# A two-layer decoder step: kept cache rows copied from input to output in the feed-forward stage, and an earlier report of GpSimd to the stage barrier

## The reference, cut to what matters

```python
# per layer, sample group (8 sequences x 4 tokens)
win_buf = cache_win_kv[l]                                  # (8, 512, 2, 2, 64)
kw = jnp.concatenate([win_buf, kv_w], axis=1)              # 512 old rows, then 4 new ones
o_w = window_attn(q, kw, q_pos, k_pos)
s_win[l] = kw[:, -512:]                                    # output: rows 4..511 of the cache, then the 4 new rows
C_new = decay * C + einsum(ws, k, v)                       # recurrent state, (8, 4, 64, 128), an output too
x = x + g1 * (concat(a_out, m_out) @ wo)                   # output projection
u, gt = split(xn2 @ w_up); y = (silu(conv(u)) * gt) @ w_down
```

## Time and profile before

| | us |
|---|---|
| median of 3 runs | 1839.16 (1837.89 to 1844.75) |
| the profiled execution's own time | 1831.91 |
| its span, first to last instruction | 1830.1 |
| TensorE busy | 1698.8 (93%) |
| VectorE busy | 919.4 (50%) |
| ScalarE busy | 610.7 (33%) |
| GpSimd busy | 187.5 (10%) |

### The profile page before, as it was taken

The page is one execution under the profiler, slowest core; times in us unless marked ns, Lnnn a source line. Parts: engine busy times, 40 slices in busy tenths (PEclk is TensorE's granted clock), DMA queues, the critical chain, the costliest instruction groups (busy, mean ns, idle before and its releaser), DMA issues.

```text
span 1830.1 us, 37052 instructions
## 1 busy us (share of the span) xinstructions
PE 1698.8 (93%) x14719; PEld 1526.7 (83%) x14719; DVE 919.4 (50%) x2374; ACT 610.7 (33%) x1165; POOL 187.5 (10%) x304
## 2 busy tenths in 40 slices
PE   5899998977989999999989999898798999999996
PEld 4799965545989999999989997645598999999995
DVE  2534434646365645546463343474545554654644
ACT  2332225634142323323152212463333332422413
POOL 1001003432000000000000100153200000000001
PEclk9899988988989999999999997898898999999998
DMA  8335278369322222221133535634861222221201
GB/s 297 118 99 181 78 273 261 115 225 200 82 76 65 92 93 93 93 92 47 49 89 90 179 102 186 221 105 137 217 114 47 92 93 93 93 92 47 93 24 54
DMA packets 157903, 219.42 MB, mean 120 GB/s; under 512 B 11722, under 2 KB 116490, under 8 KB 157548
## 3 DMA queue, kind: packets, MB, share of 16 engines
q1 hardware_dynamic: 150096, 199.22, 34.7%
q0 software_dynamic: 7648, 17.94, 3.9%
HBM read 200.45 MB, written 16.68 MB: 119 GB/s over the span
## 4 chain that ended last, share of the span: by engine, by line
PE 85%; DVE 5%; ACT 3%; SPq 2%; issue 2%; DMA 1%; POOL 1%; DVEq 1%; ACTq 0%
PE ps L1237 28%; PE ps L1263 15%; PE ps L809 13%; PE ps L1197 6%; PE ps L683 2%; PE ps L920 2%; PE ps L935 2%; PE ps L854 2%; PE ps L890 1%; PE ps L795 1%; PE ps L804 1%; PE ps L803 1%; SPq L546 1%; PE ps L1217 1%; PE ps L870 1%
## 5 line engine op out<-in xcount | busy, mean ns | idle before, releaser
L1237 PE MATMUL ps<-work_r,big_r 128*128 128x272 f32 x1344 | 279.2, 289 | 1.4 <-ACT work L1622 0.3
L1237 PE MATMUL ps<-work_r,slab_r 128*128 128x272 f32 x1344 | 278.5, 288 | 0.0
L1237 PE MATMUL ps<-xnT_r,big_r 128*128 128x272 f32 x1344 | 276.4, 287 | 0.0
L1237 PEld LDWEIGHTS ps<-work_r,big_r 128*128 128x128 f32 x1344 | 210.2, 188 | 3.9 <-issue 3.9
L809 PE MATMUL ps<-slab_r,work_r 128*128 128x256 f32 (+1 forms) x976 | 213.3, 285 | 0.0
L1237 PEld LDWEIGHTS ps<-xnT_r,big_r 128*128 128x128 f32 x1344 | 211.7, 188 | 0.0
L1237 PEld LDWEIGHTS ps<-work_r,slab_r 128*128 128x128 f32 x1344 | 210.5, 188 | 0.0
L1727 DVE TENSOR_TENSOR slab_r<-slab,big_r 128x2048 fp32r<-128x2048 f32 (+1 forms) x84 | 170.2, 2036 | 49.5 <-ACT big_r L1606 44.1
L809 PEld LDWEIGHTS ps<-slab_r,work_r 128*128 128x128 f32 x976 | 163.4, 191 | 2.7 <-issue 2.5
L1625 ACT ACTIVATE big<-big,work 128x560 f32<-128x560 f32 x44 | 33.7, 765 | 372.1 <-DVE big L2321 372.1
L1263 PE MATMUL ps<-side_r,big_r 128*128 128x272 f32 x704 | 148.3, 292 | 4.9 <-DVE big_r L1727 4.9
(11 more groups left out here) (446 smaller groups left out, 3204.9 us busy)
## 6 DMA issues: line engine op xcount, KB each, us to landing
slab<-in_w_mod SPq DMA_DIRECT2D x23, 2048.0 KB, 9.0
slab<-in_w_up SPq DMA_DIRECT2D x44, 1024.0 KB, 7.5
slab<-in_w_in SPq DMA_DIRECT2D x20, 1024.0 KB, 5.9
slab<-in_w_down SPq DMA_DIRECT2D x20, 1024.0 KB, 6.0
slab<-in_cache_cmp_kv SPq DMA_DIRECT2D x128, 128.0 KB, 2.0
slab<-in_cache_sel_kv SPq DMA_DIRECT2D x96, 128.0 KB, 2.0
big<-in_cache_win_kv SPq DMA_DIRECT2D x16, 512.0 KB, 5.2
out<-big POOLq DMA_DIRECT2D x16, 448.0 KB
```

The costliest lines, as they stand in the source:

```text
L1237: ins = mm(ps[2 * half + b][:, 0:HALF], wt, fr(x[:, k, HALF * b:HALF * b + HALF]), start=k == 0 and n == 0, stop=k == KC - 1 and n == 2)
```

## The change

Three edits. The 16 stores of window rows from `big` in the decode part of each layer are gone; in their place 8 DMAs a layer copy the same rows from the input tensor to the output tensor, issued by GpSimd in the feed-forward part behind `decode_scaled`. GpSimd adds to `stage_done` right behind the `kwb` products, ahead of its waits for `ms_Cc` and its state stores, where before it did so behind them. ScalarE's wait ahead of `split_out(0)` goes, and with it the first of the three `win_kept` reports per layer; the semaphore is now `states_kept`, with two reports per layer.

```diff
-        ST_ALL = 16 * (3 + 2 + NB + 1 + NB + 2 + 16 + 8 + 2)
+        ST_ALL = 16 * (3 + 2 + NB + 1 + NB + 2 + NB + 8 + 2)
...
-        win_kept = ctx.enter_context(nc.semaphore("window_rows_and_states_stored"))
+        states_kept = ctx.enter_context(nc.semaphore("states_and_tails_stored"))
...
                 act.wait_ge(d_pv.sem, d_pv.at(4, L))
-                act.wait_ge(win_kept, 3 * L + 1)
                 split_out(0)
...
-                    dve.wait_ge(win_kept, 3 * L)
+                    dve.wait_ge(states_kept, 2 * L)
...
-                        dve.wait_ge(win_kept, 3 * L + 2)
+                        dve.wait_ge(states_kept, 2 * L + 1)
...
-                for b in range(NB):
-                    if b % 4 == 0:
-                        pool.wait_ge(wpg_in[b // 4], L * 64 + 64)
-                    ob = by_part(s_win[L][b][0:WINDOW - NT])
-                    for lo, hi in ((1, 113), (113, 128)):
-                        put(ob[lo - 1:hi - 1], wpg[b][lo:hi].rearrange("p i c -> p (i c)"))
                 pool.wait_ge(d_s.sem, d_s.at(6, L))
...
                 ins.then_inc(ms_kb.sem, 1)
-                all_stored()
-                pool.sem_inc(win_kept, 1)
+                pool.sem_inc(stage_done, 1)
                 for s_ in range(2):
...
-                pool.sem_inc(stage_done, 1)
                 pool.wait_ge(stage_done, stage_end(12, L))
...
                 all_stored()
-                pool.sem_inc(win_kept, 1)
+                pool.sem_inc(states_kept, 1)
                 decode_scaled(2 * L + 1, 24)
+                for b in range(NB):
+                    put(by_part(s_win[L][b][0:WINDOW - NT]), by_part(A["cache_win_kv"][L][b][NT:WINDOW]))
                 pool.wait_ge(ul_c.sem, ul_c.at(6, L))
...
                 all_stored()
-                pool.sem_inc(win_kept, 1)
+                pool.sem_inc(states_kept, 1)
```

## The result

The changed kernel took 1828.2 us in the median of 8 runs (1823.71 to 1831.36), the kernel before 1836.38 in the median of 8 beside it (1829.23 to 1844.75): a ratio of 0.995, 95% interval 0.9932 to 0.9968, or 8.2 us less. The forecast was 7.7 us less. The profiled execution took 1829.4 us and its span is 1827.1 us, so between the two profiled spans only 3.0 us show.

A forecast was written before the change was run, and what follows sets the result against it. TensorE, busy 93% of the span, bounds the kernel; gains come only where it stands still. Barrier 4.6 plus page wait 3.1, all else 0, makes 7.7 us: 1839.2 to 1831.5 us, range 1825.5 to 1839.5.

The forecast's parts named there:

- Barrier, 4.6 us: Barrier behind the decode part: GpSimd reports before its state stores, VectorE becomes last; 2.3 us gained per layer.
- ScalarE's wait, 0: Ahead of split_out(0) in the decode part: its weights' landing, not GpSimd, released the split, so removal gains nothing.
- Page wait, 3.1 us: Last selected page in the decode part: without window stores SyncE's loads speed up, ending TensorE's 1.46 and 1.64 us waits.
- The clock, 0: TensorE's half clock behind the barrier: its end might move along, stay or come sooner; taken as 0, between them.
- more than the sum: Rival, chance 0.13: shorter barrier pause restores TensorE's full clock at once, 2.2 us more per layer; 12.1 us gained, 1827.1.
- Copies, 0: Start of the feed-forward part: eight copies a layer, 4.16 MB in 14.5 us, run in idle DMA engines and cost nothing.
- the 24.5 us of room: Feed-forward part: idle DMA time between the copies' issue at about 519.3 and the next loads at 543.82.
- The slow-copies rival: Feed-forward up-projection loads: copies over 32 us run beside them, landing 11.1 us late; 14.5 us slower, 1853.7; chance 0.06.
- half shares: Up-projection loads beside copies: queues alternate by packet, load gets about half, takes 15 us, 3.6 us late per layer.

The follow-up runs named there:

- barrier_alone: The kernel before with only GpSimd's report to stage_done moved right behind the kwb products, window stores and their wait kept; 1832.3 us, ratio 0.9974.
- copies_alone: The changed kernel with the report put back behind the state stores, so only window rows moved and ScalarE's wait gone; 1836.43 us, 0.9994 to the kernel before.
- before_again: The kernel before, unedited, run once more for a second profile; 1833.86 us, ratio 0.9994.
- copies_in_decode: The changed kernel with the same eight copies a layer issued in the decode part, where the window stores stood; 1842.83 us, 1.0054 to the kernel before.
- gain_wait_late: The changed kernel with VectorE's norm-gain wait moved from its first softmax division to the product using the gains; 1828.21 us, 0.9966 to the kernel before.
- filled: The changed kernel with ten unread products added in three TensorE gaps of the decode part; 1827.17 us, 0.9952 to the kernel before.
- late_first_filled: The changed kernel with VectorE's norm-gain wait later, pages loaded ahead of four window blocks, and ten unread products; 1826.77 us, 0.995 to the kernel before.

## Why the prediction was right, point by point

- *Barrier, 4.6 us.* Right. It was sized at 2.3 us a layer; the trace has 2.50 us and 2.51. Nothing of the 0.28 us that GpSimd had needed behind VectorE was left. barrier_alone gives 4.1 us by medians.
- *ScalarE's wait, 0.* Right as far as seen: in both kernels' first profiles, both layers, its split was released by the landing of its weights, behind 2.5 to 2.9 us of idleness. It was never undone by itself.
- *Page wait, 3.1 us.* The mechanism was right, the worth was not. Page loads went to 17.06 and 17.39 us (17.47 was said), TensorE's wait was gone, and its key turn came 1.4 and 1.9 us earlier. Some 12 us later a stretch at half clock took about 1.5 us back in each layer, up to the drain nothing (0.2 us lost, 0.3 won) was left, and copies_alone has no gain in time.
- *The clock, 0.* This is the term that failed. The text looked for it behind the barrier. There it gave a little: the full clock came back 3.8 and 3.0 us behind L1197's start, and 4.8 and 3.9 us before, which was worth 0.3 us a layer. The half-clock stretch around the barrier is 17.1 us long in all six decode parts with the late report (before, before_again, copies_alone) and 13.7 us in the six of the changed kernel's two profiles and barrier_alone, so the rival "more than the sum" had the direction right and not the size. What cost the term its zero lies ahead of the barrier, in thin work that the text had called unchanged: the short stretch of 3.4 us. That it follows from the closed wait is not shown.
- *Copies, 0.* Right, and sized right: 14.5 us said, 14.2 measured. They were issued at 516.8, not 519.3, in part since GpSimd's second piece of `decode_scaled` waited 0.89 us and not 2.20. One reading was off: the 24.5 us of room need 170 GB/s for 4.16 MB, and the text's 130 GB/s belong to the 32 us at which both loads would run beside the copies.
- *The slow-copies rival, 1853.7 with loads of three times their length.* The room in the schedule kept it off. Its price was nearly right where it was brought about: the load took 21.2 us (22.5 said), ScalarE's split came 9.9 us late, 11.35 of idleness in place of 1.42 (11.1 said), and the run was 12.6 us slower than the kernel before by medians (14.5 said). What was said for a small chance, half shares, was wrong; only the placement, in 24 us of idle DMA engines, protected the change.

The sum over the terms as the two profiles have it is 5.1 us in the decode parts, 6.1 over two profiles each, against 7.7 forecast and 8.2 timed, whose interval reaches from 5.9 to 12.5. The total was right partly by luck: nearly all that the profiles show is the barrier's 5.0 us, the page wait's 3.1 did not come through, and what makes up the rest of the 8.2 timed is open.

## What to carry to other kernels

Let an engine report to a barrier as soon as its own writes and reads that the next stage can harm are over, and issue its stores behind the report: that alone was half of the gain here by the times, and nearly all of it by the stages. What such stores still read needs a guard of its own; here VectorE waits for `states_kept` before it overwrites the place of `Cs`. A transfer may go where the DMA engines are idle, but look at what it would meet if it came late: the queues here shared packets and not bytes, so large contiguous copies starve loads of small rows. And where TensorE's work is thin, don't count a closed gap in full: here a wait of 1.46 and 1.64 us was closed, a stretch at half clock came 12 us behind it in each layer, and next to nothing of the gain was left at the barrier.

## What the runs showed that I had not expected

- Two queues shared the DMA engines by packets and not by bytes: 524 and 523 packets in 6 us, 1.89 and 0.52 MB; with pieces of 32512 bytes on one side 135 and 133 packets in 6 us, 2.21 and 0.14 MB.
- Eight copies from HBM to HBM in pieces of 32512 bytes moved 4.16 MB in 14.2 us, 293 GB/s (397 from 520 to 525), much as the stores from on-chip memory in pieces of 4096 bytes, 287 GB/s.
- SyncE's reads of page numbers for `big` took up to 2005 ns beside these stores (2302 in barrier_alone) and at most 276 ns beside the copies of copies_in_decode.
- A short half-clock stretch came in 12 of 12 decode parts without page wait and window stores, in 3 of 6 with both, and in the 2 of gain_wait_late with the wait alone. It was absent in both layers of `filled`, with ten unread products in TensorE's gaps, and in one of two of `late_first_filled`.
